# Two transformer blocks on one core: the sums of weight blocks are made by GpSimd in SBUF, half a group at a time, instead of by accumulating transfers in DRAM

## The chip, the cores and the metric

The kernel runs on one core of one Trainium2 chip. The time is that of the device for one execution, in microseconds (us), from the runs of the kernel; the profile is one further execution, taken by the hardware profiler. The core has TensorE (PE, matrix products), VectorE (DVE), ScalarE (ACT), GpSimd (POOL) and SyncE (SP, which here only issues transfers). All engines run their own queue of instructions in order and wait for each other through semaphores.

## What is computed

The reference runs two transformer blocks on 512 tokens of width 1024, in fp32: the first with a mixer, cross-attention over 256 memory rows and a feed-forward layer with a short convolution, the second with four mixers side by side and a feed-forward layer with a squared ReLU. Cut to the lines that matter here, the two products by large down-projections:

```
# first block, conv_ffn: w_down is [2816, 1024]
g, val = jnp.split(u, 2, axis=-1)
return (jax.nn.gelu(g) * val) @ w_down
...
# second block: mlp_w2 is [4096, 1024]
m = jnp.square(jax.nn.relu(h @ mlp_w1[l])) @ mlp_w2[l]
x = x + rms_norm(m, post_mlp_g[l])
```

## The kernel before

Every product is made in three passes, to keep fp32 accuracy out of a reduced type: an input is split into a high and a low part (`xh`, `xl`), a weight chunk of 128x1024 into `whi` and `wlo`, and PE adds high by high, low by high and high by low. A weight chunk comes by a transfer of SP into one of four `stage` buffers (line 2991), ACT casts it to `whi` (line 1862), and DVE subtracts, `wlo = stage - whi` (line 2356); there are six buffers of `whi` and `wlo`, so splits run up to six chunks ahead of PE. Inputs are split the same way, mostly in lines 1899 and 1906 on ACT and 2390 on DVE.

The order of all work is written out by the class `Plan`, one list of steps that every engine walks through in order: `mixer_one`, `cross_attention`, `conv_ffn` (products `up`, then `down`), `mixer_two` (products `in2_c`, `in2_a`, `in2_v`, `in2_d`, `in2_b`, then `out2`) and `mlp` (products `m1`, then `m2`). Beside the chunks of `mixer_two` DVE has its own work: the 31 taps of a convolution over two halves of the channels (`cf_tap`, line 2780), the logits and maxima of an attention (`mb_score`, lines 2813 and 2817), a linear recurrence (`lru_in`, `lru_b`, `lru_scan`). The mean product of the convolution (`cf_mean`, PE lines 1787 and 1788) follows the last tap, ACT's cast of its result (line 2157) and DVE's rest (line 2788). `out2` takes its inputs (`x_from`) one by one from what the mixers leave. At the boundary behind it (`boundary`) each of four token tiles is normed (`post_norm`, lines 2930 and 2933), multiplied by a gain (`gain`, line 2756) and turned by PE (`turn`, line 1679) for the products of `m1`.

The products `down` (its first 16 of 22 row tiles) and `m2` are made with seven products in place of eight of quarter size, in groups of four row tiles: 4 groups in `down` (`GROUPS`), 8 in `m2`. A group has four quarters of the weight, `s11`, `s12`, `s21`, `s22`, each 128x1024 for a group, and the seven products need four sums besides: `a = s11 + s12`, `b = s12 + s22`, `c = a + s22` and `d = c + s21` (with signs laid into the inputs). The combinations on the input side are made by DVE in `combine` (lines 2892 to 2901) and kept in tiles `rs[g]`.

The four sums are made ahead of time by GpSimd's queue (lines 3117 to 3132): for two groups at a time, four transfers of 1 MB copy quarters into the DRAM tensors `down_a` to `down_d` or `m2_a` to `m2_d` (in the profile `m_a` to `m_d`), and four more, with `accum_op=ALU.add`, add a quarter or another sum onto them. Each waits for the one before (`sums`) and for a point in PE's progress (`at(n)` on the semaphore `mm`, which PE raises by one per finished chunk): every second chunk of `up`, then of `mixer_two` and what follows. SP fetches the finished sum into `stage` like any other chunk, and waits on `sums` for it (line 2985). Nothing else runs on GpSimd but four tiny powers of 128x4 in the first mixer (line 3108). `more` is an SBUF tensor of 128x4x512 that holds four of the `rs` tiles.

The chunks are numbered as in the list `CHUNKS`; `CHUNK0` gives the first number of each product.

Of the kernel before, what the change touches and what calls it, by code (L numbers as in the profile page):

```python
# [58 lines left out]
COPIES = (("a", "s11"), ("b", "s12"), ("c", "s22"), ("d", "s21"))  # L59
ADDS = (("a", "s12"), ("b", "s22"), ("c", "a"), ("d", "c"))  # L60
# [1094 lines left out]
class Own:  # L1155
# [5 lines left out]
    def inc(self):  # L1161
# [26 lines left out]
       "ln_z", "ln_x", "xa_m", "xa_p", "lam_m", "lam", "hb", "ln_sum", "mg", "up_pad", "up_c", "up_t", "up_h", "eps6", "xn",  # L1188
# [3 lines left out]
    + ["ml_rs", "sums", "combined", "taken"])  # L1192


def build_program(nc, d, out):
    plan = Plan()
    with ExitStack() as ctx:
# [14 lines left out]
        more = sb("more", [128, 4, 512])  # L1212
# [104 lines left out]
        def moved_at(name, t):  # L1317
# [3 lines left out]
        rs = ([tiles(more[:, g, :], 2) for g in range(4)] + [tiles(reg(92 + 2 * g, 512), 2) for g in range(2)]  # L1321
              + [tiles(gb[:, 1, 512 * g:512 * g + 512], 2) for g in range(2)])
# [7 lines left out]
        def seven_x(name, i):  # L1330
            kind, g = SEVEN[name][i]
            if kind == "r3":
                return t_of(name, "t21", g)
            return t_of(name, kind, g) if kind[0] == "t" else rs[g]
# [518 lines left out]
        def _(e):  # L1853
# [227 lines left out]
            def decay():  # L2081
                q.wait_ge(S["lam_m"], 1)
                e.activation(s2, s2, ACT.Exp).then_inc(S["lam_e"])
# [151 lines left out]
            def lru_a():  # L2235
                q.wait_ge(S["lam"], 1)
# [106 lines left out]
        def _(e):  # L2343
# [259 lines left out]
            def ml_norm(h):  # L2603
# [4 lines left out]
                q.wait_ge(S["ml_rs"], h + 1)  # L2608
# [49 lines left out]
            def decay():  # L2658
# [6 lines left out]
                e.tensor_tensor(s2, s1, P("lam", 0, 2), ALU.min).then_inc(S["lam_m"])  # L2665
# [222 lines left out]
            def combine(name, kind, g):  # L2888

                if kind == "r1":  # L2890
                    q.wait_ge(S["up_h" if name == "down" else "m1_h"], 4 * g + 4)
                    v = e.tensor_tensor(rs[g], t_of(name, "t21", g), t_of(name, "t22", g), ALU.subtract)
                elif kind == "r3":
                    v = e.tensor_tensor(t_of(name, "t21", g), t_of(name, "t11", g), t_of(name, "t21", g), ALU.subtract)
                elif kind == "r2":
                    q.wait_ge(S["combined"], plan.combined_at[name, "r3", g])
                    v = e.tensor_tensor(rs[g], t_of(name, "t11", g), rs[g], ALU.subtract)
                elif kind == "r4":
                    q.wait_ge(S["combined"], plan.combined_at[name, "r2", g])
                    v = e.tensor_tensor(rs[g], t_of(name, "t12", g), rs[g], ALU.subtract)  # L2900
# [71 lines left out]
        def _(e):  # L2972
# [4 lines left out]
            def chunk(i):  # L2977
                if i < len(CHUNKS):
# [123 lines left out]
        def _(e):  # L3102
            q = Waits(e)
            for h in range(4):
# [3 lines left out]
                e.tensor_tensor(rs, rs, mhalf, ALU.pow).then_inc(S["ml_rs"])  # L3108

            def long_rows(w, part):  # L3110
                return w[2 * part:2 * part + 2].rearrange("g (r h) c -> (g r) (h c)", h=2)
# [149 lines left out]
```

## Time and profile before

| what | value |
|---|---|
| median of 3 runs | 1241.32 us (1240.67 to 1241.93) |
| the profiled execution | 1241.24 us |
| its span, first to last instruction | 1239.4 us |
| PE busy | 1232.1 us, 99% |
| DVE busy | 851.0 us, 69% |
| ACT busy | 627.6 us, 51% |
| GpSimd busy | 39.7 us, 3% |
| transfers on GpSimd's queue (q0) | 50.33 MB |
| granted TensorE clock, mean | 1.00 |

The span is what the trace covers; about 1.8 us of the execution lie around it. A busy share is the time in which an instruction of the engine ran; whether a busy engine sets the end is read from its waits. In rows of the trace, a line such as `L2356 DVE TENSOR_TENSOR wlo<-stage,whi 128x1024` is an instruction at line 2356 of the kernel that writes `wlo` and reads `stage` and `whi`; tiles cut out of the large SBUF tensor `R` all go by that name, and all PSUM banks by `bank`. `PE bank L1813` as a releaser is PE's instruction at that line.

### The profile page before, as it was taken

The numbers are of one execution on the slowest core, as the hardware profiler recorded it, in microseconds if no ns is written. First come the engines' busy times: TensorE is split into PE (matmuls) and PEld (weight loads), VectorE is DVE, ScalarE is ACT, GpSimd is POOL, SyncE is SP. The second block draws the span as 40 slices with busy tenths as digits, with TensorE's granted clock in tenths as the row PEclk, the third lists the DMA queues.
The fourth block names the chain that finished last, engine by engine and source line by source line (L and its number), as shares of the span: only waits on it lengthen the run. The fifth ranks groups of instructions, "written<-read, shape, count | busy, mean of one in ns | idle before, by whom it ended". The sixth has DMA issues, their size and how long they took to land.

```text
span 1239.4 us, 16104 instructions
## 1 busy us (share of the span) xinstructions
PE 1232.1 (99%) x6230; PEld 1036.8 (84%) x6230; DVE 851.0 (69%) x1227; ACT 627.6 (51%) x1050; POOL 39.7 (3%) x56
## 2 busy tenths in 40 slices
PE   9999999999999999999999999999999999999998
PEld 9877898898889888888888898778898888888886
DVE  5778888575577656655688588887574444477886
ACT  5565654254446444444566464568343332355664
POOL 0000001000000000000000000000000000000000
PEclk9999999999999999999999999999999999999999
DMA  8346445422236685675676337456578576265562
GB/s 288 137 146 204 143 137 176 147 70 85 85 102 205 203 191 201 183 198 196 186 256 187 101 114 222 165 130 156 187 218 222 192 196 162 97 206 201 171 208 98
DMA packets 57925, 209.88 MB, mean 169 GB/s; under 512 B 6228, under 2 KB 13908, under 8 KB 51448
## 3 DMA queue, kind: packets, MB, share of 16 engines
q1 hardware_dynamic: 50504, 158.11, 38.7%
q0 software_dynamic: 6912, 50.33, 16.6%
q8 instruction: 50, 0.82, 0.3%
q10 hardware_dynamic: 432, 0.39, 0.1%
q14 instruction: 27, 0.22, 0.1%
HBM read 200.95 MB, written 56.10 MB: 207 GB/s over the span
## 4 chain that ended last, share of the span: by engine, by line
PE 99%; DMA 0%; DVE 0%; ACT 0%; issue 0%; DVEq 0%
PE bank L1424 18%; PE bank L1425 18%; PE bank L1426 18%; PE bank L1630 6%; PE bank L1628 6%; PE bank L1629 6%; PE bank L1568 2%; PE bank L1569 2%; PE bank L1570 2%; PE bank L1571 2%; PE bank L1573 2%; PE bank L1572 2%; PE bank L1679 1%; PE bank L1743 1%; PE bank L1729 1%; PE bank L1510 1%
## 5 line engine op out<-in xcount | busy, mean ns | idle before, releaser
L1424 PE MATMUL bank<-xh,whi 128*128 128x512 f32 (+1 forms) x1136 | 413.8, 364 | 0.3 <-issue 0.2
L1425 PE MATMUL bank<-xl,whi 128*128 128x512 f32 (+1 forms) x1136 | 409.9, 361 | 0.0
L1426 PE MATMUL bank<-xh,wlo 128*128 128x512 f32 (+1 forms) x1136 | 409.8, 361 | 0.0
L2356 DVE TENSOR_TENSOR wlo<-stage,whi 128x1024 fp32r<-128x1024 f32 (+1 forms) x258 | 311.0, 1211 | 106.4 <-ACT whi L1862 105.6
L1862 ACT CAST whi<-stage 128x1024 fp32r<-128x1024 f32 (+1 forms) x258 | 266.3, 1039 | 69.9 <-PE bank L1630 28.9
L1424 PEld LDWEIGHTS bank<-xh,whi 128*128 128x128 f32 x1136 | 214.4, 189 | 37.6 <-issue 5.5
L1426 PEld LDWEIGHTS bank<-xh,wlo 128*128 128x128 f32 x1136 | 214.4, 189 | 32.8
L1425 PEld LDWEIGHTS bank<-xl,whi 128*128 128x128 f32 x1136 | 214.5, 189 | 32.0 <-issue 0.2
L1628 PE MATMUL bank<-whi,xh 128*128 128x512 f32 x328 | 127.6, 389 | 0.0
L1629 PE MATMUL bank<-wlo,xh 128*128 128x512 f32 x328 | 127.6, 389 | 0.0
L1630 PE MATMUL bank<-whi,xl 128*128 128x512 f32 x328 | 127.6, 389 | 0.0
L2955 DVE TENSOR_TENSOR R<-bank,R 128x512 f32<-128x512 f32 x32 | 22.1, 691 | 82.4 <-ACT R L2325 82.4
L2325 ACT ACTIVATE R<-bank 128x512 f32<-128x512 f32 x32 | 19.1, 598 | 110.7 <-PE bank L1426 110.7
L1630 PEld LDWEIGHTS bank<-whi,xl 128*128 128x128 f32 x328 | 61.6, 188 | 12.8
L1629 PEld LDWEIGHTS bank<-wlo,xh 128*128 128x128 f32 x328 | 61.6, 188 | 12.8
L1628 PEld LDWEIGHTS bank<-whi,xh 128*128 128x128 f32 x328 | 61.6, 188 | 12.8
L2728 DVE SCALAR_TENSOR_TENSOR R<-R,par 128x512 f32<-128x512 f32 x44 | 33.0, 751 | 53.5 <-ACT R L2103 53.5
L2100 ACT COPY R<-bank 128x512 f32<-128x512 f32 x44 | 25.8, 587 | 83.3 <-PE bank L1426 83.3
L2390 DVE TENSOR_TENSOR xl<-R,xh 128x512 fp32r<-128x512 f32 x76 | 51.1, 684 | 3.6 <-ACT xh L1899 2.7
L2780 DVE SCALAR_TENSOR_TENSOR R<-R,par 128x512 f32<-128x512 f32 x60 | 41.6, 744 | 1.6 <-ACT R L2146 1.4
L1568 PE MATMUL bank<-whi,xh 128*128 128x512 f32 x102 | 40.2, 395 | 0.0
L1569 PE MATMUL bank<-whi,xh 128*128 128x512 f32 x102 | 39.7, 389 | 0.0
(387 smaller groups left out, 1577.5 us busy)
## 6 DMA issues: line engine op xcount, KB each, us to landing
stage<-in_W_m SPq DMA_DIRECT2D x56, 512.0 KB, 4.0
stage<-in_W_up SPq DMA_DIRECT2D x44, 512.0 KB, 4.1
stage<-in_W_in_a SPq DMA_DIRECT2D x19, 512.0 KB, 3.7
stage<-in_W_down SPq DMA_DIRECT2D x18, 512.0 KB, 4.1
stage<-in_W_out SPq DMA_DIRECT2D x16, 512.0 KB, 3.9
m_a<-in_W_m POOLq DMA_DIRECT2D x8, 1024.0 KB, 8.3
m_b<-in_W_m POOLq DMA_DIRECT2D x8, 1024.0 KB, 7.5
stage<-in_W_in_b SPq DMA_DIRECT2D x10, 512.0 KB, 5.4
```

Source lines behind the costliest of these rows:

```text
L1424: e.matmul(b[:, cols], hi[:, k, :], xh[:, k, cols], start=(k == 0), stop=False)
L1425: e.matmul(b[:, cols], hi[:, k, :], xl[:, k, cols], start=False, stop=False)
L1426: last = e.matmul(b[:, cols], lo[:, k, :], xh[:, k, cols], start=False, stop=(k == 7))
L1568: e.matmul(b[0][:], a_hi, hi[:, 0:512], start=(k == 0), stop=False, skip_group_check=seeded)
L1569: e.matmul(b[1][:], a_hi, hi[:, 512:1024], start=(k == 0), stop=False, skip_group_check=seeded)
L1628: e.matmul(b[:], x[:, c], hi, start=new, stop=False, skip_group_check=True)
L1629: e.matmul(b[:], x[:, c], lo, start=False, stop=False, skip_group_check=True)
L1630: last = e.matmul(b[:], z[:, c], hi, start=False, stop=end, skip_group_check=True)
L1862: e.copy(whi[:, plan.place[i], 0:width(i)], stage[:, s, 0:width(i)]).then_inc(S["w_hi"])
L2356: e.tensor_tensor(wlo[:, plan.place[i], c], stage[:, i % NSTAGE, c], whi[:, plan.place[i], c].bitcast(F32), ALU.subtract).then_inc(S["w_lo"])
L2390: e.tensor_tensor(lo, source_of(name, k), hi.bitcast(F32), ALU.subtract).then_inc(S["x_lo"])
L2780: v = e.scalar_tensor_tensor(out=cy[c], in0=cz[c][:, k:k + 512], scalar=P("cdw", 2 * k + c), in1=cy[c], op0=ALU.mult, op1=ALU.add)
```

## The change

GpSimd no longer adds in DRAM. The 12 groups are cut into halves of 512 columns, 24 in all (`SUMMED`). For each half it loads the four quarters into the SBUF tensor `parts` (the former `more`), adds them with four instructions of 128x512, in place, and stores the four results to the DRAM tensors. It waits for the point `at(n)` and for the stores of the half before, then for its loads (`s_in`), and for its own adds where one reads what another wrote (`p_own`). The points are now every third chunk of `up` for the first 14 halves and every second of `mixer_two` for the other ten. SP waits for the stores of both halves of a group. The `rs` tiles that lay in `more` move to free places in `R` and `gb`. To stay within the number of semaphores, `ml_rs` is replaced by `p_own`, and `lam_m` by the first count of `lam`.

The core of the diff:

```
-        more = sb("more", [128, 4, 512])
+        parts = sb("parts", [128, 4, 512])
...
-        rs = ([tiles(more[:, g, :], 2) for g in range(4)] + [tiles(reg(92 + 2 * g, 512), 2) for g in range(2)]
-              + [tiles(gb[:, 1, 512 * g:512 * g + 512], 2) for g in range(2)])
+        rs = {"down": [tiles(reg(60 + 2 * g, 512), 2) for g in range(4)],
+              "m2": [tiles(reg(92 + 2 * g, 512), 2) for g in range(2)]
+                    + [tiles(gb[:, 1 + g // 2, 512 * (g % 2):512 * (g % 2) + 512], 2) for g in range(4)]
+                    + [tiles(reg(88 + 2 * g, 512), 2) for g in range(2)]}
...
-                            q.wait_ge(S["sums"], 16 * (8 * (g // 2) + 5 + "abcd".index(kind) + (16 if n == "m2" else 0)))
+                            q.wait_ge(S["sums"], 64 * (SUMMED.index((n, g, 1)) + 1))
...
             def at(n):
-                return CHUNK0["up"] + 2 * n + 1 if n < 22 else CHUNK0["in2_c"] + 2 * (n - 22) + 1
-
-            n = 0
-            for block in ("down", "m2"):
-                for part in range(GROUPS[block] // 2):
-                    for name, w in COPIES:
-                        q.wait_ge(S["mm"], at(n))
-                        if n:
-                            q.wait_ge(S["sums"], 16 * n)
-                        e.dma_start(long_rows(sums[block, name], part), long_rows(quarter(block, w), part),
-                                    max_dma_last_dim=8192).then_inc(S["sums"], 16)
-                        n += 1
-                    for name, w in ADDS:
-                        q.wait_ge(S["mm"], at(n))
-                        q.wait_ge(S["sums"], 16 * n)
-                        added = sums[block, w] if w in "ac" else quarter(block, w)
-                        e.dma_start(long_rows(sums[block, name], part), long_rows(added, part), accum_op=ALU.add,
-                                    max_dma_last_dim=8192).then_inc(S["sums"], 16)
-                        n += 1
+                if n < 14:
+                    return CHUNK0["up"] + 1 + 3 * n
+                return CHUNK0["in2_c"] + 1 + 2 * (n - 14)
+
+            for n, (block, g, hf) in enumerate(SUMMED):
+                cols = slice(512 * hf, 512 * hf + 512)
+                q.wait_ge(S["mm"], at(n))
+                if n:
+                    q.wait_ge(S["sums"], 64 * n)
+                for i, w in enumerate(QUARTERS):
+                    e.dma_start(parts[:, i, :], quarter(block, w)[g][:, cols]).then_inc(S["s_in"], 16)
+                q.wait_ge(S["s_in"], 64 * n + 64)
+                s11, s12, s21, s22 = (parts[:, i, :] for i in range(4))
+                e.tensor_tensor(s11, s11, s12, ALU.add).then_inc(S["p_own"])
+                q.wait_ge(S["p_own"], 4 * n + 4 + 1)
+                e.tensor_tensor(s12, s12, s22, ALU.add).then_inc(S["p_own"])
+                e.tensor_tensor(s22, s22, s11, ALU.add).then_inc(S["p_own"])
+                q.wait_ge(S["p_own"], 4 * n + 4 + 3)
+                e.tensor_tensor(s21, s21, s22, ALU.add).then_inc(S["p_own"])
+                q.wait_ge(S["p_own"], 4 * n + 4 + 4)
+                for name, made in (("a", s11), ("b", s12), ("c", s22), ("d", s21)):
+                    e.dma_start(sums[block, name][g][:, cols], made).then_inc(S["sums"], 16)
```

On PE and SP the instructions and their order are the same before and after, on ACT and DVE as well but for the names of the `rs` tiles. GpSimd's queue before, for the first two groups of `down` (`in_W_down` is the weight in DRAM, the waits in brackets):

```order
L3123 DMA down_a<-in_W_down 128x2048 [waits mm]
L3123 DMA down_b<-in_W_down 128x2048 [waits sums,mm]
L3123 DMA down_c<-in_W_down 128x2048 [waits sums,mm]
L3123 DMA down_d<-in_W_down 128x2048 [waits sums,mm]
L3130 DMA down_a<-in_W_down 128x2048 [waits sums,mm]
L3130 DMA down_b<-in_W_down 128x2048 [waits sums,mm]
L3130 DMA down_c<-down_a 128x2048 [waits sums,mm]
L3130 DMA down_d<-down_c 128x2048 [waits sums,mm]
```

These are all that GpSimd does for two groups: eight transfers, and no instruction on data.

GpSimd's queue after, for the first half of the first group of `down` and the head of the next half:

```order
L3122 DMA parts<-in_W_down 128x512 [waits mm]
L3122 DMA parts<-in_W_down 128x512 x3
L3125 TENSOR_TENSOR parts<-parts 128x512 [waits s_in]
L3127 TENSOR_TENSOR parts<-parts 128x512 [waits p_own]
L3128 TENSOR_TENSOR parts<-parts 128x512
L3130 TENSOR_TENSOR parts<-parts 128x512 [waits p_own]
L3133 DMA down_a<-parts 128x512 [waits p_own]
L3133 DMA down_b<-parts 128x512
L3133 DMA down_c<-parts 128x512
L3133 DMA down_d<-parts 128x512
L3122 DMA parts<-in_W_down 128x512 [waits sums,mm]
```

Four transfers in, four additions in SBUF and four transfers out now stand for each half of a group, with waits between them; the same rows stand 24 times, with `m2` in place of `down` from the ninth on.

## Rows read from the trace of the kernel before

**Rows 1.** The page: span, and the busy time of each engine.
```profile
span 1239.4 us, 16104 instructions
...
PE 1232.1 (99%) x6230; PEld 1036.8 (84%) x6230; DVE 851.0 (69%) x1227; ACT 627.6 (51%) x1050; POOL 39.7 (3%) x56
```

**Rows 2.** Waits of PE, 3 to 1230 us: us in total, times, longest.
```profile
PE bank L1464 <- ACT xh L1869: 0.3, 1, 0.3
PE bank L1424 <- issue: 0.2, 1, 0.2
```

**Rows 3.** Windows: length, DVE busy (instructions), granted clock, DMA share, GB/s.
```profile
385.00:545.00 160.00, 96.50 (x115) 1.00 0.71 204
...
620.00:705.00 85.00, 64.24 (x81) 1.00 0.62 198
...
746.00:811.00 65.00, 52.44 (x82) 1.00 0.58 181
811.00:836.50 25.50, 23.97 (x37) 1.00 0.58 140
...
847.00:864.00 17.00, 16.71 (x23) 1.00 0.68 163
```

**Rows 4.** Timeline of GpSimd at 740 us; SP's fetches of sums, first to last.
```profile
740.52 0.81 POOL L3130 DMA_DIRECT2D m_c<-m_a  x1 [131.31 <-PE bank L1426]
...
L2991 SPq DMA_DIRECT2D stage<-down_a x4: 319/323/327, 570.5 to 627.2; - x4
...
L2991 SPq DMA_DIRECT2D stage<-m_a x8: 319/320/327, 1035.5 to 1135.7; - x8
```

**Rows 5.** The page, DMA issues: count, KB each, median us to landing.
```profile
stage<-in_W_m SPq DMA_DIRECT2D x56, 512.0 KB, 4.0
...
m_a<-in_W_m POOLq DMA_DIRECT2D x8, 1024.0 KB, 8.3
```

**Rows 6.** Groups by form, DVE, 811 to 868 us: busy us, mean ns.
```profile
L2780 DVE SCALAR_TENSOR_TENSOR R<-R,par 128x512 f32<-128x512 f32 x20 | 13.9, 745 | 0.1
L2356 DVE TENSOR_TENSOR wlo<-stage,whi 128x1024 fp32r<-128x1024 f32 x9 | 10.9, 1218 | 1.1 <-ACT whi L1862 1.1
...
L2872 DVE TENSOR_TENSOR R<-bank,R 128x512 f32<-128x512 f32 x2 | 1.4, 690 | 0.3
...
L2858 DVE TENSOR_TENSOR R<-R 128x512 f32<-128x512 f32 x2 | 1.3, 686 | 0.0
```

**Rows 7.** Timelines of GpSimd and DVE, 155 and 170 us: start, length.
```profile
155.23 1.07 POOL L3108 TENSOR_TENSOR st<-st,par 128x4 f32<-128x4 f32 x1 [154.78 <-DVE st L2601]
...
155.32 0.68 DVE L2539 SCALAR_TENSOR_TENSOR R<-R 128x512 f32<-128x512 f32 x1
...
170.13 1.23 DVE L2356 TENSOR_TENSOR wlo<-stage,whi 128x1024 fp32r<-128x1024 f32 x1
...
170.31 1.92 POOL L3108 TENSOR_TENSOR st<-st,par 128x4 f32<-128x4 f32 x1 [14.02 <-DVE st L2601]
```

**Rows 8.** Timelines of DVE, ACT and PE at three places.
```profile
834.93 1.53 DVE L2780 SCALAR_TENSOR_TENSOR R<-R,par 128x512 f32<-128x512 f32 x2
...
839.57 1.14 ACT L2157 CAST whi<-R 128x512 fp32r<-128x512 f32 x2
...
842.49 0.39 PE L1787 MATMUL bank<-whi,first 128*128 128x512 f32 x1
...
863.14 0.68 DVE L2390 TENSOR_TENSOR xl<-R,xh 128x512 fp32r<-128x512 f32 x1
...
864.25 0.39 PE L1568 MATMUL bank<-whi,xh 128*128 128x512 f32 x1
...
895.32 1.23 DVE L2756 TENSOR_TENSOR R<-R,gb 128x1024 f32<-128x1024 f32 x1
...
896.89 1.03 PE L1679 MATMUL bank<-ident,R 128*128 128x128 f32 x8
```

More of the change, by code:

```diff
@@ L58 @@
 QUARTERS = ["s11", "s12", "s21", "s22"]
-COPIES = (("a", "s11"), ("b", "s12"), ("c", "s22"), ("d", "s21"))
-ADDS = (("a", "s12"), ("b", "s22"), ("c", "a"), ("d", "c"))
+SUMMED = [(block, g, hf) for block in GROUPS for g in range(GROUPS[block]) for hf in range(2)]
 M2_TILES = [2, 3, 0, 1]
@@ L1187 @@
        "swa_logit", "swa_nm", "swa_r", "swa_tr", "qk_c", "qk_s", "o_s", "ml_set", "ml_d", "ml_w", "ml_n", "ml_rv", "ml_h", "ml_y",
-       "ln_z", "ln_x", "xa_m", "xa_p", "lam_m", "lam", "hb", "ln_sum", "mg", "up_pad", "up_c", "up_t", "up_h", "eps6", "xn",
+       "ln_z", "ln_x", "xa_m", "xa_p", "lam", "hb", "ln_sum", "mg", "up_pad", "up_c", "up_t", "up_h", "eps6", "xn",
        "cf_z", "cf_taps", "cf_s", "cf_y", "mb_logit", "mb_m", "mb_r", "mb_y", "lru_c", "lru_i", "lru_m",
        "lru_h", "sc_p", "sc_y", "m1_h", "pn_w", "pn_x", "r2", "last"]
-    + ["ml_rs", "sums", "combined", "taken"])
+    + ["p_own", "sums", "s_in", "combined", "taken"])
 def build_program(nc, d, out):
@@ L1333, in seven_x @@
                 return t_of(name, "t21", g)
-            return t_of(name, kind, g) if kind[0] == "t" else rs[g]
+            return t_of(name, kind, g) if kind[0] == "t" else rs[name][g]
         source = {"out1": hT, "down": hid1, "out2": yT, "m2": hid2}
@@ L2081, in decay @@
             def decay():
-                q.wait_ge(S["lam_m"], 1)
+                q.wait_ge(S["lam"], 1)
                 e.activation(s2, s2, ACT.Exp).then_inc(S["lam_e"])
@@ L2235, in lru_a @@
             def lru_a():
-                q.wait_ge(S["lam"], 1)
+                q.wait_ge(S["lam"], 2)
                 q.wait_ge(S["lru_c"], 2)
@@ L2607, in ml_norm @@
                 mv = st[:, c + 16:c + 24].rearrange("p (i c) -> p i c", i=4)
-                q.wait_ge(S["ml_rs"], h + 1)
+                q.wait_ge(S["p_own"], h + 1)
                 for i in range(4):
@@ L2664, in decay @@
                 after()
-                e.tensor_tensor(s2, s1, P("lam", 0, 2), ALU.min).then_inc(S["lam_m"])
+                e.tensor_tensor(s2, s1, P("lam", 0, 2), ALU.min).then_inc(S["lam"])
                 q.wait_ge(S["lam_e"], 1)
@@ L2896, in combine @@
                     q.wait_ge(S["combined"], plan.combined_at[name, "r3", g])
-                    v = e.tensor_tensor(rs[g], t_of(name, "t11", g), rs[g], ALU.subtract)
+                    v = e.tensor_tensor(rs[name][g], t_of(name, "t11", g), rs[name][g], ALU.subtract)
                 elif kind == "r4":
                     q.wait_ge(S["combined"], plan.combined_at[name, "r2", g])
-                    v = e.tensor_tensor(rs[g], t_of(name, "t12", g), rs[g], ALU.subtract)
+                    v = e.tensor_tensor(rs[name][g], t_of(name, "t12", g), rs[name][g], ALU.subtract)
                 else:
@@ L3107, in _ @@
                 q.wait_ge(S["ml_rv"], h + 1)
-                e.tensor_tensor(rs, rs, mhalf, ALU.pow).then_inc(S["ml_rs"])
-            def long_rows(w, part):
-                return w[2 * part:2 * part + 2].rearrange("g (r h) c -> (g r) (h c)", h=2)
+                e.tensor_tensor(rs, rs, mhalf, ALU.pow).then_inc(S["p_own"])
             def at(n):
-                return CHUNK0["up"] + 2 * n + 1 if n < 22 else CHUNK0["in2_c"] + 2 * (n - 22) + 1
-            n = 0
-            for block in ("down", "m2"):
-                for part in range(GROUPS[block] // 2):
-                    for name, w in COPIES:
-                        q.wait_ge(S["mm"], at(n))
-                        if n:
-                            q.wait_ge(S["sums"], 16 * n)
-                        e.dma_start(long_rows(sums[block, name], part), long_rows(quarter(block, w), part),
-                                    max_dma_last_dim=8192).then_inc(S["sums"], 16)
-                        n += 1
-                    for name, w in ADDS:
-                        q.wait_ge(S["mm"], at(n))
-                        q.wait_ge(S["sums"], 16 * n)
-                        added = sums[block, w] if w in "ac" else quarter(block, w)
-                        e.dma_start(long_rows(sums[block, name], part), long_rows(added, part), accum_op=ALU.add,
-                                    max_dma_last_dim=8192).then_inc(S["sums"], 16)
-                        n += 1
```

2 lines of the change are left out of this document (1 added, 1 removed).

## The prediction, made before the changed kernel ran

> **What bounds the kernel now.** I read the busy shares first: PE works 1232.1 of 1239.4 us [rows 1]. A busy PE is no proof of a full one, so I went on to what PE waited for: between 3 and 1230 us its idle time is 0.3 + 0.2 us, in two waits [rows 2]. So the number of matmuls sets the time, at a granted clock of 1.00 in every window [rows 3], and the change leaves PE's instructions and their order as they are. What it can save in the middle is at most those 0.5 us: the forecast is then a question of what it can cost, and where PE has next to no margin over its suppliers. The supplier to look at is DVE, since it makes the low half of every weight chunk and of every input, and GpSimd gets work that reads SBUF beside it. DVE is busy 0.60 of the time beside the `up` product, but 0.81 from 746 to 811 us, 0.94 from 811 to 836.5 and 0.98 from 847 to 864 [rows 3].
>
> **The change part by part.**
>
> *Removed:* 48 accumulating or plain transfers of 1 MB on GpSimd's queue. Nobody waits for them before the result is fetched, so taking them away frees no engine. Their reader is SP, which asks for the four `down_a` sums from 570.5 to 627.2 us and for those of `m2` from 1035.5 [rows 4].
>
> *Added, per half group, 24 times:* four loads of 256 KB, four adds of 128x512, four stores of 256 KB, each set behind the last, all on GpSimd's own queue. Behind its new waits stands only its own later work; who waits for that is SP, for the sums. Renamed semaphores and the new places of the r tiles keep count and order on DVE and ACT: nothing.
>
> *How long a half takes.* The trace has no such transfer into SBUF from GpSimd. SP lands 512 KB in 4.0 us, GpSimd's own 1 MB takes 8.3 us [rows 5]; four loads together are 1 MB from a software queue, four stores as well, and I take 6 us for each, between the ends. An add has no row either. DVE does the same shape, two SBUF operands, in 0.69 us [rows 6]; the longest add of GpSimd, with only 4 columns, shows 1.92 [rows 7]. I take the middle, 1.3 us. Four adds, each behind one DVE instruction of about 0.7 us, make 8 us. So a half takes 6 + 8 + 6 = 20 us (ends 4.0 + 5.6 + 4.0 = 14 and 8.3 + 10.5 + 8.3 = 27).
>
> The Trainium skill ("GPSIMD Engine Reference", section "Performance versus the Vector engine") puts a two-input add of 2048 fp32 columns at 4497 ns. As an estimate a quarter of it is 1.12 us, and by it a half would take 19 us and the sum below would be 4.2 us in place of 7.4, since stretches 2 and 3 would then cost nothing. No run here shows it.
>
> *Are the sums late?* The first eight halves start at 385 us, on a trigger every three chunks or every 20 us, and end by 385 + 8 x 20 = 545, before SP's first request at 570.5. The ten halves from 740.5 us on (GpSimd's issue at that trigger: [rows 4]) end by 740.5 + 200 = 941, before 1036. Even at 27 us a half they end by 1011, and the eight of `down` by 601, with the last group's wanted at 627. Cost nothing.
>
> *What an add does to DVE.* At 170.13 us DVE starts a split, which reads `stage` and `whi`, both in SBUF. GpSimd's add starts at 170.31 and shows 1.92 us; the one at 155.23 shows 1.07 [rows 7]. The extra 0.85 us is close to what was left of the split. So the two exclude each other while both read SBUF, at least where DVE came first. Where GpSimd came first (155.23, DVE's two-operand instruction at 155.32) DVE still took its 0.68 us, but with 4 columns there was nothing to hold it. I take it that a 512-column add holds a DVE instruction with two SBUF operands for its whole length.
>
> This is what the Trainium skill says ("SBUF — State Buffer", section "Who interferes with whom"): such a DVE instruction and a GpSimd one that reads SBUF share a read port, and the second to come waits for the other to end. By that rule, the forecast holds; without it, the first rival does. The trace agrees for one of the two directions.
>
> *The price.* From 811 to 868 us the forms that read two SBUF operands, headed by the taps (13.9 us) and the splits (10.9), make 0.87 of DVE's busy time; the rest reads a PSUM bank, as L2872 does, or is small [rows 6]. So a half costs DVE 4 x 1.3 x 0.87 = 4.5 us where it is busy throughout, and 0.81 of that, 3.7, from 746 to 811. What of it reaches PE, by stretch:
>
> 1. Beside `up` and the start of `down` (14 halves, 385 to 665): DVE idles 0.40 of the time in the one and 0.24 in the other [rows 3], 8 and 4.9 us in 20, both more than 4.5. Splits and inputs run up to six chunks ahead of PE, and that is the work that hides it; in `down`, where only 0.4 us is left over per half, a late step would be paid at once. Cost 0.
> 2. 746 to 811: adds at about 747, 767, 787 and the start of 807, four halves: 4 x 3.7 = 14.8 us against 12.6 idle. Cost 2.
> 3. 811 to 836.5: the end of that fourth half and one whole, 1.44 x 4.5 = 6.5 us, against 1.5 idle. DVE's last tap comes 5.0 us later than its 836.46. Behind the tap stand ACT's cast (from 839.57), DVE's rest and PE's mean product at 842.49 [rows 8]. The chain itself needs about 0.62 + 0.69 + 0.3 for the handoffs, so the tap has 4.4 us of room. Cost 0.6.
> 4. 847 to 864: one half, 4.5 us, against 0.3 idle. Here DVE is one unbroken queue, and its rest for chunk 1 of `out2` ends at 863.82, with PE's first product from it at 864.25 [rows 8]: 0.4 us of room. Cost 3.8.
> 5. 885 to 915, the boundary behind `out2`: DVE's gain product ends at 896.55, PE's turn starts at 896.89 [rows 8], 0.3 us of room, and a chain of this kind stands before each turn. Two halves fall there; inside the chains DVE also waits for ACT, and most of a held piece falls into such a wait, so of 2 x 4.5 us I take 1.
>
> Sum: 2 + 0.6 + 3.8 + 1 = 7.4 us. The profiled execution took 1241.24 us with a span of 1239.4, the median is 1241.32, 0.08 above it: forecast 1248.7.
>
> The ends: with adds of 0.69 us and halves of 14 us, stretch 2 costs nothing, stretches 3 and 4 see 3.8 halves of 2.4 us against 6.6 us of idle and room, together about 2.5. With adds of 1.92 and halves of 18 to 27 us, stretches 2 to 5 give 9 to 23.
>
> **The rivals.**
>
> *DVE isn't held, or only for moments (not slower).* If a long GpSimd add and a DVE read share the port by turns, or the read runs ahead of the add, DVE loses some tenths of a microsecond per half and the 12.6, 4.4 and 0.4 us above swallow nearly all. The DVE instruction at 155.32 that kept its 0.68 us speaks for it; GpSimd's 0.85 us of waiting speaks against it. It decides from a loss of under about 2 us a half. Time: 1241.3 to 1242.
>
> *DVE becomes the bound (heavy).* Where each add holds for 1.92 us and transfers take only 4 us, a half costs 6.7 us of every 18: 3.6 halves x 5.4 = 19.5 against 12.6 in stretch 2, and 2.9 x 6.7 = 19.5 against 6.6 in 3 and 4, with 3 at the boundary: some 23 us, 1264. It decides from a loss of about 6 us a half; for it speaks GpSimd's 1.92 us, against it that part of that was waiting.
>
> *Faster.* The accumulating transfers move the same 50 MB but read their target in DRAM too; if they slowed SP's loads of weights, those would land sooner. But PE waits for no load: 0.5 us in all is to be had [rows 2]. 1240.8 at best.
>
> *Late sums.* SP's queue is in order, so a sum that isn't there holds every later weight. That takes halves of over 30 us (eight from 385 to 627); 27 was the worst above. The eighth would then come late by the eight-fold of what a half is over 30, so at 31 some 8 us, 1249, no worse than the forecast.
>
> *It doesn't do what it says.* The order of GpSimd's queue shows the four loads, adds and stores per half; I give this nothing.
>
> **How the numbers follow.** Forecast case, +2.5 to +13 us: 0.60. DVE not held: 0.25. Heavy: 0.10. Faster: 0.03. Late sums: 0.02. A measurement here can tell about 0.2%, 2.5 us, from no change. Slower by more than that is the forecast case but for its lowest edge, the heavy case and the late sums: 0.70. Within it: the second case with the edge, 0.27. Faster: 0.03. The range runs from the case of no hold, 1241.0, to 1257.0, past the middle of what the price bounds give, and leaves out most of the heavy case and the faster one.
>
> **What would show it.** In the profile after, the adds on `parts` last 1.1 to 1.9 us each, and a group of four is spaced by DVE's instructions. DVE's taps (L2780's form) have a mean above 745 ns, or gaps before them, in 740 to 870 us only where adds run; splits beside `up` stretch as well without any wait of PE. PE shows waits for DVE's `xl` or `wlo` at the mean product and at `out2`, and at the turns before `m1`. If PE's waits stay under 1 us and the DVE forms keep their means, the hold was wrong. If DVE's are longer and PE still doesn't wait, the room was larger than I read it. If SP waits for GpSimd, the sums were late after all.

## The result, and the profile after

The changed kernel takes 1262.83 us (median of 4, 1258.64 to 1268.17) beside 1241.5 for the kernel before in the same rounds: the ratio is 1.0175, 95% interval 1.0131 to 1.0219. It is slower by 21 us where I had forecast 7.4, and lies past the end of my range. The profiled execution is the longest of the four, 1268.17 us with a span of 1266.4, 27.0 more than the span before, so its rows show more than the median's loss. The page of it, span and busy time of each engine:

```profile
span 1266.4 us, 16318 instructions
...
PE 1242.5 (98%) x6230; PEld 1041.7 (82%) x6230; DVE 921.6 (73%) x1227; ACT 627.2 (50%) x1050; POOL 272.4 (22%) x296
```

DVE does the same 1227 instructions and is busy 70.6 us longer than in [rows 1], 2.9 us for each half. PE does the same 6230 and is busy 10.4 us longer. The rest of the loss is waiting. Waits of PE, 3 to 1230 us, in total, times, longest:

```profile
PE bank L1629 <- DVE R L2907: 5.5, 1, 5.5
PE bank L1680 <- DVE R L2757: 4.3, 3, 2.7
PE bank L1569 <- DVE R L2887: 3.1, 1, 3.1
PE bank L1803 <- DVE R L2814: 2.1, 1, 2.1
PE bank L1569 <- DVE first L2398: 0.9, 1, 0.9
PE bank L1629 <- DVE wlo L2357: 0.5, 1, 0.5
PE bank L1465 <- ACT xh L1870: 0.2, 1, 0.2
...
```

[Rows 2] had 0.5 us in all; this view, with two more waits of 0.2, adds up to 17. So 10.4 us of slower matmuls and some 16.5 us of new waits make the 27.0, and nothing else is left. Every new wait of any size names DVE, though behind DVE something else can stand (stretch 5 below). Windows of the kernel after, to be held against [rows 3] (length, busy time of PE, its weight loads, DVE, ACT and GpSimd with counts, granted clock, DMA share, GB/s):

```profile
385.00:545.00 160.00, 160.00 (x730) 133.43 (x729) 117.02 (x114) 78.37 (x109) 80.26 (x88) 1.00 0.61 200
620.00:705.00 85.00, 79.00 (x335) 64.25 (x334) 72.84 (x77) 47.05 (x63) 36.56 (x41) 0.96 0.81 281
746.00:811.00 65.00, 64.98 (x414) 54.70 (x414) 58.68 (x75) 33.28 (x61) 31.13 (x34) 1.00 0.57 193
811.00:836.50 25.50, 23.44 (x115) 17.64 (x115) 22.39 (x31) 11.41 (x25) 12.13 (x16) 0.93 0.49 168
```

Beside `up` (first row) DVE is busy 20.5 us longer and PE loses nothing. Beside `down` (second row) PE loses 6.0 us, with DVE busy only 0.86 of the time. The cause of DVE's longer time is plain in the two timelines from 638 us on, in `down` (start, length):

```profile
638.10 1.42 POOL L3125 TENSOR_TENSOR parts<-parts 128x512 f32<-128x512 f32 x1 [7.80 <-DMA parts<-in_W_m]
639.59 1.62 POOL L3127 TENSOR_TENSOR parts<-parts 128x512 f32<-128x512 f32 x1
641.17 2.28 POOL L3128 TENSOR_TENSOR parts<-parts 128x512 f32<-128x512 f32 x1
643.53 1.62 POOL L3130 TENSOR_TENSOR parts<-parts 128x512 f32<-128x512 f32 x1
...
638.28 1.79 DVE L2391 TENSOR_TENSOR xl<-R,xh 128x512 fp32r<-128x512 f32 x1
639.99 2.32 DVE L2357 TENSOR_TENSOR wlo<-stage,whi 128x1024 fp32r<-128x1024 f32 x1
642.23 1.78 DVE L2391 TENSOR_TENSOR xl<-R,xh 128x512 fp32r<-128x512 f32 x1
643.93 2.31 DVE L2357 TENSOR_TENSOR wlo<-stage,whi 128x1024 fp32r<-128x1024 f32 x1
```

L2391 normally takes 0.69 us and L2357 1.22; each is 1.1 us longer here, once per addition. The additions are longer too (1.27 us is the shortest of the L3125 ones): the engines alternate, one instruction each. Four turns cost DVE 4.4 us a half where it has no gap between its instructions.

What PE does behind its longest wait, PE's timeline from 657 us on:

```profile
657.89 0.39 PE L1631 MATMUL bank<-whi,xl 128*128 128x512 f32 x1
...
663.76 0.76 PE L1629 MATMUL bank<-whi,xh 128*128 128x512 f32 x1 [5.48 <-DVE R L2907]
664.32 0.63 PE L1630 MATMUL bank<-wlo,xh 128*128 128x512 f32 x1
664.75 0.63 PE L1631 MATMUL bank<-whi,xl 128*128 128x512 f32 x1
```

Matmuls start every 0.43 us in place of every 0.227, and the granted clock of 663 to 669 us is 0.50: TensorE was granted 1.2 GHz, not 2.4, until 669.4 us. Over the whole execution the mean granted clock is 0.992. The other three executions had 0.998, 0.994 and 0.998 with spans of 1258.4, 1263.6 and 1256.8: the spread of the kernel's times goes with that clock.

### The profile page after: what moved, and what is told of

Read it like the earlier page. It is cut to its first block, busy times and chain, and to the rows that moved or that the text cites. A ratio compares the mean times of both kernels' runs of the same rounds, so it can differ in the third digit from the quotient of the medians.

```text
span 1266.4 us, 16318 instructions
## 1 busy us (share of the span) xinstructions
PE 1242.5 (98%) x6230; PEld 1041.7 (82%) x6230; DVE 921.6 (73%) x1227; ACT 627.2 (50%) x1050; POOL 272.4 (22%) x296
## 4 chain that ended last, share of the span: by engine, by line
PE 83%; DVE 10%; ACT 2%; issue 2%; DMA 2%; SPq 0%; DVEq 0%; ACTq 0%
PE bank L1425 16%; PE bank L1426 16%; PE bank L1427 16%; PE bank L1629 5%; PE bank L1631 5%; PE bank L1630 5%; DVE R L2781 3%; DVE wlo L2357 2%; PE bank L1569 2%; PE bank L1572 2%; PE bank L1570 2%; PE bank L1574 2%; PE bank L1571 2%; PE bank L1573 2%; PE bank L1680 1%
## 5 line engine op out<-in xcount | busy, mean ns | idle before, releaser
L2357 DVE TENSOR_TENSOR wlo<-stage,whi 128x1024 fp32r<-128x1024 f32 (+1 forms) x258 | 328.2, 1277 | 100.7 <-ACT whi L1863 99.9
L1629 PE MATMUL bank<-whi,xh 128*128 128x512 f32 x328 | 129.2, 394 | 6.0 <-DVE R L2907 5.5
L2391 DVE TENSOR_TENSOR xl<-R,xh 128x512 fp32r<-128x512 f32 x92 | 71.6, 793 | 11.0 <-ACT xh L1900 10.1
L1629 PEld LDWEIGHTS bank<-whi,xh 128*128 128x128 f32 x328 | 62.2, 190 | 20.1 <-issue 5.9
L3122 POOL DMA_DIRECT2D parts<-in_W_down x32 | 17.6, 555 | 218.1 <-PE bank L1427 180.0
L1900 ACT CAST xh<-R 128x512 fp32r<-128x512 f32 x70 | 42.3, 616 | 44.7 <-DVE R L2898 22.4
L3122 POOL DMA_DIRECT2D parts<-in_W_m x64 | 34.8, 550 | 126.8 <-DMA m_d<-parts 64.0
L3125 POOL TENSOR_TENSOR parts<-parts 128x512 f32<-128x512 f32 x24 | 33.3, 1386 | 130.7 <-DMA parts<-in_W_m 90.9
```

Source lines behind the costliest of these rows:

```text
L1629: e.matmul(b[:], x[:, c], hi, start=new, stop=False, skip_group_check=True)
L1900: e.copy(tiles(xh[:, k % 8, :], 2), source_of(name, k)).then_inc(S["x_hi"])
L2357: e.tensor_tensor(wlo[:, plan.place[i], c], stage[:, i % NSTAGE, c], whi[:, plan.place[i], c].bitcast(F32), ALU.subtract).then_inc(S["w_lo"])
L2391: e.tensor_tensor(lo, source_of(name, k), hi.bitcast(F32), ALU.subtract).then_inc(S["x_lo"])
L3122: e.dma_start(parts[:, i, :], quarter(block, w)[g][:, cols]).then_inc(S["s_in"], 16)
```

## The experiments

My theory was that the additions hold DVE and that PE pays where DVE has no room. There were two suspects before the first four runs, the additions and the 96 + 96 small transfers that go with them, and one doubt: whether a GpSimd instruction of any kind does the harm, or one that reads SBUF. The line numbers of these kernels can be off by a few from the changed one's.

**Transfers without additions.**

```
-                e.tensor_tensor(s11, s11, s12, ALU.add).then_inc(S["p_own"])
...
-                e.tensor_tensor(s21, s21, s22, ALU.add).then_inc(S["p_own"])
-                q.wait_ge(S["p_own"], 4 * n + 4 + 4)
```

> The changed kernel without its 96 additions: GpSimd loads the quarters into SBUF and stores them unchanged, so the sums (and the output) are not computed; every transfer of the change remains. Theory A, an addition of GpSimd holds DVE instructions that read two SBUF operands: without additions DVE's instructions keep their lengths of before (split 1.22 us, tap 0.745 us) and the time is that of before, 1240 to 1243 us. Rival B, the transfers through GpSimd's queue into SBUF slow SP's loads or DVE: the time stays above 1252 us.

1241.23 us, ratio 1.0001 (0.9992 to 1.0011), DVE busy 851.3. The loads and stores cost nothing by themselves.

**Additions without transfers.**

```
-                for i, w in enumerate(QUARTERS):
-                    e.dma_start(parts[:, i, :], quarter(block, w)[g][:, cols]).then_inc(S["s_in"], 16)
...
-                    e.dma_start(sums[block, name][g][:, cols], made).then_inc(S["sums"], 16)
```

> The changed kernel without GpSimd's transfers: the 96 additions run on a zeroed SBUF tensor at points of PE's progress chosen near the times at which they ran in the changed kernel; SP fetches a plain quarter where it fetched a sum, so the output is not the reference's. Theory A: DVE's total busy time stays near 920 us as in the changed kernel (851 before), PE waits for DVE 8 to 18 us in all, and the time is 1250 to 1268 us. Rival B (transfers): 1240 to 1243 us.

1264.71 us, ratio 1.0186 (1.0170 to 1.0201), DVE busy 918.2, PE 1241.4, clock 0.991. The additions alone make the whole loss: 23.6 us over the kernel before, with the points placed by hand near the old times, and the longest wait, for L2907, is there as well (6.0 us).

**Write-only fills in place of the additions.**

```
+                for r in range(3):
+                    for t in (s11, s12, s22, s21):
+                        last = e.memset(t, 0.0)
+                    last.then_inc(S["p_own"])
+                    q.wait_ge(S["p_own"], 4 + 3 * n + r + 1)
```

> The changed kernel with each group of four additions replaced by twelve GpSimd fills of 128x512, which write SBUF but read nothing; the sums are left out, the transfers remain. Theory A in its narrow form (the shared thing is the reading of SBUF): DVE keeps its lengths and the time is 1240 to 1243 us although GpSimd is busy. Rival C (any GpSimd instruction on SBUF holds DVE): DVE's instructions stretch as in the changed kernel, over 1250 us.

1243.23 us, ratio 1.0015 (1.0006 to 1.0024). GpSimd is about as busy as in the changed kernel, but DVE is not touched. From its page, busy times and the two groups that the additions had stretched (busy, mean ns):

```profile
PE 1232.1 (99%) x6230; PEld 1036.3 (84%) x6230; DVE 851.2 (69%) x1227; ACT 627.8 (51%) x1050; POOL 249.2 (20%) x488
...
L2357 DVE TENSOR_TENSOR wlo<-stage,whi 128x1024 fp32r<-128x1024 f32 (+1 forms) x258 | 311.1, 1211 | 104.5 <-ACT whi L1863 103.7
...
L2391 DVE TENSOR_TENSOR xl<-R,xh 128x512 fp32r<-128x512 f32 x92 | 61.7, 686 | 11.0 <-ACT xh L1900 10.1
```

In the kernel before the split's group has a mean of 1211 ns too, in the changed kernel the two groups have 1277 and 793 ns. So it is the reading of SBUF, not GpSimd's being busy. The 2 us of the median over the kernel before stay unexplained: the one profiled execution, in which PE waits 0.9 us, is among the shortest of the ten (1241.71 us) and can't show all of them. It shows 0.5 us of them at L1680, the boundary, and so do three runs below (`up` only, `down` only and the one-operand reads). In these four the slowest of SP's transfers `R<-gb` there lands after 3.4 to 3.7 us, in the runs at 1241 us after 2.6 to 2.8; stretch 5 at the end comes back to them. Three of the runs below fill as well, so I hold these runs against 1243.2 too.

**The transfers of before with all else of the change.** The new semaphores, and the new places of the `rs` tiles, which I had priced at nothing:

```
-            for n, (block, g, hf) in enumerate(SUMMED):
...
+            for block in ("down", "m2"):
...
+                        e.dma_start(long_rows(sums[block, name], part), long_rows(added, part), accum_op=ALU.add,
```

> The changed kernel with the accumulating transfers of before put back, so that only the new places of the r tiles and the renamed semaphores remain. Theory A: nothing of these has a cost, 1240 to 1243 us. A rival by which the r tiles in their new places cost time would show a time above 1244 us.

1241.11 us, ratio 1.0001 (0.9991 to 1.0010). Nothing, as priced.

The next question was where. Three kernels add in one region only and fill elsewhere; the fourth keeps every addition and moves it.

```
+                if n < 10:
+                    e.tensor_tensor(s11, s11, s12, ALU.add).then_inc(S["p_own"])
...
+                else:
+                    for r in range(4):
+                        for t in (s11, s12, s22, s21)[r == 3:]:
+                            last = e.memset(t, 0.0)
+                        last.then_inc(S["p_own"])
+                        q.wait_ge(S["p_own"], 4 * n + 4 + r + 1)
```

**Additions beside `up` only.**

> Only the ten halves beside the up product (n below 10) add their blocks; the other fourteen make 15 write-only fills in place of their four additions, so their sums are wrong while every transfer stays. First theory (each addition holds a DVE instruction that reads SBUF twice, and only room in DVE's day hides it): DVE gains about 10 x 2.9 = 29 us of busy time, and since it idles 0.40 of the time there, PE waits under 1 us more: 1241 to 1242.5. Rival (a held DVE is paid everywhere, in small pieces, that would be 10/24 of the loss): 1250 to 1252.

1242.96 us, ratio 1.0013 (1.0004 to 1.0023), as with fills alone. DVE is busy 873.1, 22 us longer, and PE does not notice.

**Additions beside `down` only**, the condition being `10 <= n < 14`.

> Only the four halves beside the down product (n = 10 to 13) add; the other twenty make write-only fills in place of the additions, so their sums are wrong. In the changed kernel PE waited 6.0 us here, and behind its long wait its matmuls ran at half their pace for some 6 us. First theory (waits and the granted clock behind them both count): 6 us of waits and about 3 us of clock, 1249 to 1251. Rival (only the waits count): 1247 at most. If the idle time of DVE beside down were room, as I had forecast, under 1243.

1248.81 us, ratio 1.0067 (1.0050 to 1.0084). In its profile PE is busy 1234.8 us, 2.7 more than before, and waits 3.1 us for L2907 and 0.6 at L1629. So waits and clock both count, as the first theory said, but the time is just below its 1249 to 1251. The waits are smaller than the changed kernel's 6.0 us: here the same two halves add some 3 to 5 us earlier, and the combination that PE waits for comes 5.4 us late instead of 8.0.

**Additions from the mixer on only**, `n >= 14`.

> Only the ten halves from the projections of the second mixer on (n from 14) add; the other fourteen make write-only fills in place of the additions, so their sums are wrong. In the changed kernel PE waited about 10.6 us from there on. First theory: those waits and 4 to 7 us of granted clock behind them, 1255 to 1259, and this run and the one with the down halves alone add up to the whole loss of 21 to 23 us within 3 us. Rival (the lag of the one part is carried into the other, so the parts don't add): the two losses together differ from it by over 5 us.

1258.88 us, ratio 1.0137 (1.0121 to 1.0154). Its waits of PE are at the places of the changed kernel's from 700 us on, but longer: 6.2 us at L1680 in place of 4.3, 3.1 at L1569 for L2887, 2.1 at L1803 and some small ones, 15.9 in all where the changed kernel has 10.6. PE is busy only 3.2 us longer. At L1569 PE waits for L2887 as long in both profiled executions, until 872.78 us here (3.07 us) and until 881.67 us in the changed kernel (3.08 us). The windows of these waits differ in the clock (this run, then the changed kernel; columns as above):

```profile
870.00:880.00 10.00, 6.26 (x25) 4.65 (x26) 9.89 (x12) 5.59 (x9) 4.44 (x3) 1.00 0.71 242
...
880.00:890.00 10.00, 8.33 (x30) 6.68 (x31) 9.93 (x11) 4.48 (x8) 5.63 (x4) 0.83 0.72 249
```

Against the run with fills the three parts cost -0.3, 5.6 and 15.7 us, 21.0 together; the changed kernel's loss is 21.3. The parts add, as far as the median of four executions from 1258.6 to 1268.2 us can tell.

**All additions, in other places.**

```
-                if n < 14:
-                    return CHUNK0["up"] + 1 + 3 * n
-                return CHUNK0["in2_c"] + 1 + 2 * (n - 14)
+                first = {0: ("out1", 0), 1: ("xq", 0), 5: ("up", 1), 15: ("down", 26), 16: ("m1", 0)}
+                name, c = first[max(k for k in first if k <= n)]
+                return CHUNK0[name] + c
```

> The changed kernel, complete, with all additions, but the halves stand elsewhere: one beside out1 (from 209 us), four beside the cross attention's query and output products (from 265), ten beside up (from 385), one at the end of down (about 690), eight beside m1 (from 920, where DVE is busy 0.45 of the time). None beside down's first part, the mixer or the boundary. First theory (place decides): DVE gains as much as in the changed kernel (about 70 us) and PE waits under 3 us more than before: 1241 to 1245. Rival (the number of additions decides, not their place): 1258 or more. Late sums would show as waits of PE for wlo beside m2.

1240.66 us, ratio 0.9995 (0.9986 to 1.0005): no slower than before, with all 96 additions on GpSimd. Its page, and all that PE waits for from 3 to 1230 us:

```profile
span 1239.4 us, 16299 instructions
...
PE 1232.0 (99%) x6230; PEld 1036.7 (84%) x6230; DVE 893.2 (72%) x1227; ACT 626.8 (51%) x1050; POOL 265.1 (21%) x296
...
PE bank L1425 <- issue: 0.2, 1, 0.2
PE bank L1465 <- ACT xh L1870: 0.2, 1, 0.2
```

DVE is still busy 42 us longer, less than the 70 I had expected. At 1.1 us each that is an estimated 38 of the 96 additions that held a DVE instruction, where 64 did in the changed kernel: more of them met a DVE that idled. Not one of those 42 us reaches PE. Windows of this kernel beside `up` and beside `m1`:

```profile
385.00:600.00 215.00, 215.00 (x971) 178.92 (x971) 156.04 (x152) 102.66 (x144) 110.65 (x120) 1.00 0.60 200
...
905.00:1075.00 170.00, 170.00 (x827) 143.94 (x825) 90.44 (x99) 57.20 (x82) 86.36 (x96) 1.00 0.62 205
```

In the first DVE's busy share rises from 0.60 (128.7 us before) to 0.73, and PE is busy for all of it. From 620 to 680 us, beside `down`, DVE is busy 50.77 of 60 us, exactly as in the kernel before, since no addition runs there.

**The clock by itself.** Two kernels make the sums as before and let PE wait for GpSimd's fills inside `down`, with no DVE held:

```
+                if name == "down" and i in PAUSES:
+                    q.wait_ge(S["p_own"], 4 + ROUNDS * (PAUSES.index(i) + 1))
...
+                            for m, i in enumerate(PAUSES):
+                                q.wait_ge(S["mm"], CHUNK0["down"] + i)
+                                for r in range(ROUNDS):
+                                    for t in range(3):
+                                        last = e.memset(parts[:, t, :], 0.0)
+                                    last.then_inc(S["p_own"])
```

> No additions: the accumulating transfers of before make the sums (complete and right). At one place of the down product (its chunk 16) PE waits until GpSimd has made 9 write-only fills of 128x512, begun when PE has finished chunk 15, so PE idles some 5 us there. First theory (behind a wait of this length TensorE is granted half its clock for some 6 us, 3 us lost): 1241.3 + 5 + 3, that is 1248.5 to 1250. Rival (half pace behind the wait in the changed kernel came from something else, the held DVE for one): 1246 to 1247.

1249.07 us, ratio 1.0064 (1.0049 to 1.0079), 8.1 us more than before, for one wait. Its page, its wait, and its windows on both sides of it:

```profile
PE 1234.1 (99%) x6230; PEld 1037.9 (83%) x6230; DVE 851.7 (68%) x1227; ACT 627.8 (50%) x1050; POOL 44.0 (4%) x65
...
PE bank L1632 <- POOL parts L3138: 4.8, 1, 4.8
...
650.00:660.00 10.00, 7.15 (x32) 5.60 (x30) 8.74 (x13) 6.41 (x10) 2.73 (x6) 1.00 0.60 178
660.00:670.00 10.00, 8.02 (x28) 6.49 (x29) 5.94 (x8) 3.33 (x5) 1.64 (x4) 0.83 0.24 86
670.00:680.00 10.00, 10.00 (x46) 8.26 (x44) 7.49 (x9) 5.13 (x7) 0.00 (x0) 1.00 0.67 188
```

PE waits 4.8 us, and then the granted clock of the next 10 us is 0.83. The profiled run lost 4.8 + 2.0 us (PE is busy 2.0 longer); the median lost 8.1. DVE has nothing to do with it.

> As the kernel with one long wait, but PE waits at three places of the down product, 22 us apart (chunks 8, 16 and 24), each time for 3 write-only fills, some 1.8 us each. First theory (the clock falls only behind long waits; in the changed kernel waits under 1.5 us left it at 1.00): the waits alone, 1241.3 + 5.4, 1246.5 to 1247.5. Rival (each wait costs clock, however short): 1250 or more.

1248.4 us, ratio 1.0054 (1.0039 to 1.0069), between the two expectations. The profiled run bears the first out: three waits, 5.2 us in all, clock 1.00, span 1244.5, 5.1 more than before. The other three runs had a clock of 0.998 and spans of 1246.5 to 1246.8, 2 us longer. Waits of 1.8 us cost clock in some executions and not in others; no trace shows at which of the three.

**How long the hold is, and for what.** The last two change the reads themselves.

```
-                e.tensor_tensor(s11, s11, s12, ALU.add).then_inc(S["p_own"])
+                e.tensor_scalar(s11, s12, 1.0, None, ALU.mult).then_inc(S["p_own"])
```

(and the other three in the same way, with one wait more)

> The changed kernel with each of the four additions of a half replaced by a product with 1.0 of one block (one operand read in SBUF, 128x512), so the sums are wrong. Transfers and places are the same. First theory (a GpSimd instruction that reads SBUF takes the port whatever the number of its operands, for its length): DVE's splits and remainders get longer as in the changed kernel, in proportion to these instructions' length; with some 0.6 us in place of 1.3, half of the loss, 1250 to 1254. Rival (only two-operand reads of GpSimd exclude DVE): as with the write-only fills, 1243 to 1244.

1243.22 us, ratio 1.0020 (1.0010 to 1.0029). The time is the rival's, the reason is not. Timelines of GpSimd and DVE, 635 to 640 us:

```profile
635.93 2.07 POOL L3127 TENSOR_SCALAR parts<-parts 128x512 f32<-128x512 f32 x1
638.08 2.07 POOL L3129 TENSOR_SCALAR parts<-parts 128x512 f32<-128x512 f32 x1
...
635.44 1.21 DVE L2357 TENSOR_TENSOR wlo<-stage,whi 128x1024 fp32r<-128x1024 f32 x1
636.57 1.09 DVE L2391 TENSOR_TENSOR xl<-R,xh 128x512 fp32r<-128x512 f32 x1
637.59 1.21 DVE L2357 TENSOR_TENSOR wlo<-stage,whi 128x1024 fp32r<-128x1024 f32 x1
```

L2391 takes 1.09 us in place of 0.69, L2357 its usual 1.21. So an instruction with one operand in SBUF holds DVE as well, but for 0.40 us in place of 1.1, and DVE gets two instructions through beside each. DVE's busy time grows by 16.8 us in all, and of that the wait for L2907 shows 1.0 us and one other 0.4: a quarter of the hold costs PE almost nothing beyond what the run with fills costs, where my first theory had the loss in proportion.

I had expected these products to be short, some 0.6 us. They aren't: at 941.56 us, while DVE idles, one takes 1.49 us, more than an addition (1.27 to 1.29). So the hold doesn't follow the length of GpSimd's instruction, and of the 2.07 us beside a busy DVE only some 0.6 are waiting.

**The additions in four pieces.**

```
+                for p in range(4):
+                    c = slice(128 * p, 128 * p + 128)
+                    at_ = 16 * n + 4 * p + 4
+                    e.tensor_tensor(s11[:, c], s11[:, c], s12[:, c], ALU.add).then_inc(S["p_own"])
```

(and the other three in the same way)

> The changed kernel, complete, with each addition made in four pieces of 128 columns (16 GpSimd instructions a half). First theory (the held time is the read time of all additions, however cut): at least the loss of the changed kernel, 1259 to 1268. Rival (shorter holds are absorbed in DVE's handoffs): 1245 to 1255.

1245.95 us, ratio 1.0034 (1.0020 to 1.0049). I had expected the full loss; 5 us of 21 are left. Timelines, 644 to 647 us:

```profile
643.19 1.49 POOL L3128 TENSOR_TENSOR parts<-parts 128x128 f32<-128x128 f32 x1
644.75 0.79 POOL L3130 TENSOR_TENSOR parts<-parts 128x128 f32<-128x128 f32 x1
645.51 1.44 POOL L3131 TENSOR_TENSOR parts<-parts 128x128 f32<-128x128 f32 x1
...
644.26 0.96 DVE L2391 TENSOR_TENSOR xl<-R,xh 128x512 fp32r<-128x512 f32 x1
645.15 1.48 DVE L2357 TENSOR_TENSOR wlo<-stage,whi 128x1024 fp32r<-128x1024 f32 x1
646.55 0.95 DVE L2391 TENSOR_TENSOR xl<-R,xh 128x512 fp32r<-128x512 f32 x1
```

Each DVE instruction is now 0.26 us longer, not 1.1. The read time of a half is the same, 16 x 0.26 = 4.2 us, but DVE's busy time grows by only 30 us over the kernel (1.3 us a half). GpSimd waits for DVE at many pieces (the four lines have means of 0.69 to 0.76 us, the shortest take 0.45) and a half takes some 27 us in place of 22, so the holds come thinner in time. It is the second expectation that holds. Whether the shorter hold or the thinner row of holds counts more, these runs don't separate; PE still waits 2.5 us for L2907, in `down`.

## Why the prediction was wrong, point by point

- **What bounds the kernel, nothing to gain, nobody else touched**: right. Transfers by themselves, renamed semaphores and new places cost nothing, and SP waited for no sum. Stretch 5 has the one place where the transfers do add something.
- **How long a half takes**: 20 us forecast, 19 to 25 measured from the loads of one to those of the next, 22 in the mean. An alone-standing addition takes 1.27 to 1.29 us, I had taken 1.3 (the estimate from the Trainium skill, "GPSIMD Engine Reference", section "Performance versus the Vector engine", was 1.12).
- **The hold**: right in kind, and close in size. DVE's instruction waits 1.1 us for an addition, 4.4 us a half where DVE never idles; I had 4.5, from a hold of 1.3 us and a share of 0.87 of such instructions, so that the two agree so well is in part luck. The trace now agrees in both directions with the rule that I drew from the Trainium skill ("SBUF — State Buffer", section "Who interferes with whom"), and with its other half, that a GpSimd instruction which only writes does not exclude such a DVE instruction: 1211 and 686 ns beside fills. It doesn't agree that the second always waits for the other to end, as I had put it: the product of 1.49 us holds DVE for 0.40.
- **Stretches 2 to 4, the mixer**: 6.4 us forecast, 6.3 of waits measured (2.1 at 829.7, 0.2 at 856.7, 0.9 at 875.6, 3.1 at 881.7). That agreement is luck in part. Stretch 2 cost nothing: over the same 65 us of work, 755.7 to 820.7 us now, DVE is busy 61.0 us in place of 52.4, which is 8.6 more where I had 14.8 against 12.6 of idle time, and PE doesn't wait. The 2.1 us came behind it, at the attention's products (L1803). I had 3.8 at chunk 1 of `out2`, and 4.0 came at its chunk 0, where PE waits for L2398 and then for a bank that DVE empties in L2887; here DVE was one unbroken queue, as forecast.
- **Stretch 1, "beside `up` and the start of `down`, cost 0"**: right for `up`, and the first step that failed for `down`. Two halves with additions, at 614 to 621 and 638 to 645 us, put DVE's combination `v` (L2907 of after, L2906 of before) 8.0 us later. DVE's timeline before, then after:

```profile
654.35 1.28 DVE L2906 TENSOR_TENSOR R<-R,bank 128x512 f32<-128x512 f32 x2 [0.29 <-PE bank L1630]
...
637.14 1.23 DVE L2357 TENSOR_TENSOR wlo<-stage,whi 128x1024 fp32r<-128x1024 f32 x1 [1.42 <-ACT whi L1863]
...
662.33 1.28 DVE L2907 TENSOR_TENSOR R<-R,bank 128x512 f32<-128x512 f32 x2
```

The first half made DVE 4.4 us late, and none of it was made up before the second. There 1.5 us more were lost, at 637, to a cast of ACT that itself had waited 1.7 us for a transfer of weights; the second half added 4.4. Of these 10.3 us DVE made up 2.3 before `v`, and PE waited 5.5 us. I had counted 4.9 us of idle time per half as room. Where DVE idles there, it is mostly in gaps of 0.3 to 0.7 us for ACT's casts, which come again behind the late work. Made up were mostly two gaps of 0.89 us, in which ACT's casts had waited for PE before the change. The late transfer is no condition: without GpSimd's transfers PE waits 6.0 us at this place. I had written that a late step would be paid at once in `down`, and priced it at nothing all the same.
- **Stretch 5, the boundary**: 1 us forecast, 4.3 measured, in three waits at L1680 (0.2, 2.7, 1.4). I had assumed that most of a held piece falls into DVE's waits for ACT. The additions did hold the chain itself (the gain at 925.97 us takes 2.17 us in place of 1.22, the two splits at 929.26 us 4.54 in place of 2.35). But a turned tile also comes back by four transfers of SP (`R<-gb`), and there the change's own transfers come in. These transfers and ACT's cast behind them, before, then after:

```profile
891.75 2.50 SPq L3071 DMA_DIRECT2D R<-gb  x4
896.25 1.05 ACT L1937 CAST xh<-R 128x1024 fp32r<-128x1024 f32 x1 [4.05 <-DMA R<-gb]
...
913.37 3.62 SPq L3072 DMA_DIRECT2D R<-gb  x4
920.05 1.05 ACT L1938 CAST xh<-R 128x1024 fp32r<-128x1024 f32 x1 [7.54 <-DMA R<-gb]
```

The cast starts 6.7 us behind the first issue in place of 4.5, and DVE waits for it. GpSimd's four stores of a half are issued from 912.74 us on, beside SP's. With additions and no transfers the cast starts 4.5 us behind the issue again, and L1680 waits 2.2 us in all; without additions the stores don't fall together with it and nothing is late. So about half of the 4.3 us is the stores' doing at a place to which the additions shifted them. That is read from one profiled execution of each kernel, and no run moves the stores alone.
- **The term that was missing**: PE's clock. I added up waits only. Behind them PE ran at 1.2 GHz for a while, 10.4 us of the profiled run, and the kernel with one wait of 4.8 us and an untouched DVE lost 8.1 us in the median. With the waits of this execution forecast right the sum would still have been short. The two terms are not independent, though. The changed kernel's profiled execution is 9.7 us late at the end of `down` (L2628 there starts at 707.58 us in place of 697.87) and lost the other 17.3 behind it, 10.6 in waits and by difference 6.7 in clock. The run with additions from the mixer on, whose clock stayed at 1.00 behind the same wait of 3.1 us, lost 15.4 us in new waits and 3.2 in slower matmuls. Where PE ran slower, DVE was less late for it. That is read from two executions and not tested by itself.
- **The rivals**: of the one at 1264 us the time came, not the mechanism. It wanted holds of 1.92 us; they were 1.1. "Not held" fell with the first timeline, "faster" and "late sums" did not come.

## What to carry to other kernels

A busy share of 0.75 says nothing of room until it is known whether the idle time stands in one piece behind queued work, or in handoffs of a chain: in this kernel only a supplier that ran ahead of its reader absorbed a hold. Beside `up` and `m1` the same additions cost nothing, beside `down` and the mixer 21 us, and moving them took one edit of a trigger. And where PE is the bound, a wait can cost more than its length: put a price for the granted clock beside each wait of some microseconds.

## What the runs showed of the hardware that I had not expected

- GpSimd and DVE exclude each other when GpSimd reads SBUF and DVE's instruction reads it twice, and with additions of 512 columns they alternate, one instruction each. DVE's price goes with the kind of GpSimd's instruction and not with its length: 1.1 us with additions of 512 columns (1.27 to 1.29 us long by themselves), 0.40 with a product of one operand and a constant (1.49), 0.26 with additions of 128 columns (0.45), none with write-only fills (0.52).
- One wait of 4.8 us cost 2.0 to 4.2 us besides, going by the spans of four executions (1246.2 to 1248.4, less 1239.4 and the wait, if it was as long in each; one was traced). In the changed kernel spans of 1256.8 to 1266.4 go with mean clocks of 0.998 to 0.992: the same kernel loses different amounts from one execution to the next. With the additions from the mixer on the spans don't go with the clock: 1258.2 at 0.999, 1254.1 at 0.997.
- Three waits of 1.8 us lost no clock in one execution and some 2 us in three others.
- The slowest of SP's transfers `R<-gb` landed 4.7 us after its issue where GpSimd's stores were issued beside it, and 2.7 to 2.8 at most in the kernel before and in the runs without additions or without transfers.
